# Turning the merged halves in 32 wide blocks: SyncE moves them, VectorE turns them, TensorE no longer does

## What is computed

```python
for l in range(2):
    h = rms_norm(x, mix_norm_g[l])
    z = h @ w_in[l]
    y_a = gmlp_branch(...) @ gm_w_proj[l]
    y_b = mla_branch(...) @ mla_w_proj[l]
    gates = sigmoid(z[..., OFF_GATE:].reshape(B, S, 2, D))
    merged = gates[..., 0, :] * y_a + gates[..., 1, :] * y_b     # (256, 1024)
    x = x + merged @ w_out[l]
    h2 = rms_norm(x, ffn_norm_g[l])
    x = x + (swiglu(h2, ...) if l % 2 == 0 else moe_swiglu(h2, ...))
```

## Time and profile before

| | us |
|---|---|
| median of 3 runs | 1414.58 |
| lowest, highest | 1413.52, 1414.61 |
| profiled execution | 1415.23 |
| its span, first to last instruction | 1413.5 |
| TensorE busy | 1404.5 (99%) |
| VectorE busy | 1167.7 (83%) |
| ScalarE busy | 950.0 (67%) |
| GpSimd busy | 172.1 (12%) |
| granted TensorE clock, mean | 0.999 |

### The profile page before, as it was taken

The page is one execution under the profiler, slowest core; times in us unless marked ns, Lnnn a source line. Parts: engine busy times, 40 slices in busy tenths (PEclk is TensorE's granted clock), DMA queues, the critical chain, the costliest instruction groups (busy, mean ns, idle before and its releaser), DMA issues.

```text
span 1413.5 us, 19089 instructions
## 1 busy us (share of the span) xinstructions
PE 1404.5 (99%) x6567; PEld 1159.6 (82%) x6567; DVE 1167.7 (83%) x1197; ACT 950.0 (67%) x966; POOL 172.1 (12%) x305
## 2 busy tenths in 40 slices
PE   9999999999999999999999999999999999999998
PEld 7888778888888888788888888888888888888886
DVE  6998766676557899667989898898988988999986
ACT  6678645445435677644777777777777777778774
POOL 2032003476600050000300000000000000000010
PEclk9999999999999999999999999999999999999999
DMA  9476549976666484558999999999999999999995
GB/s 338 163 217 207 179 150 332 300 228 201 200 222 206 155 245 128 194 179 314 330 355 410 365 396 408 373 390 405 351 410 372 385 405 365 393 371 393 409 374 188
DMA packets 171636, 424.32 MB, mean 300 GB/s; under 512 B 19436, under 2 KB 50792, under 8 KB 171544
## 3 DMA queue, kind: packets, MB, share of 16 engines
q1 hardware_dynamic: 157128, 393.42, 76.7%
q0 software_dynamic: 13376, 26.16, 6.1%
q10 hardware_dynamic: 1040, 3.68, 0.6%
HBM read 398.20 MB, written 15.81 MB: 293 GB/s over the span
## 4 chain that ended last, share of the span: by engine, by line
PE 96%; DMA 2%; DVE 1%; ACT 0%; SPq 0%; issue 0%; DVEq 0%; ACTq 0%
PE ps L619 89%; DMA raw_more<-in_moe_w_down 1%; PE ps L1194 1%; PE ps L1053 1%; PE ps L1062 1%; PE ps L932 1%; PE ps L1051 1%; PE ps L1037 1%; PE ps L1010 0%; PE ps L976 0%; DMA raw<-in_w_in 0%; DVE w_lo L554 0%; ACT w_hi L549 0%; PE ps L1035 0%; PE ps L1186 0%; SPq L537 0%
## 5 line engine op out<-in xcount | busy, mean ns | idle before, releaser
L554 DVE TENSOR_TENSOR w_lo<-raw,w_hi 128x2048 fp32r<-128x2048 f32 (+3 forms) x184 | 383.7, 2092 | 78.0 <-ACT w_hi L549 76.9
L549 ACT ACTIVATE w_hi<-raw 128x2048 fp32r<-128x2048 f32 (+3 forms) x184 | 322.2, 1758 | 123.7 <-PE ps L619 97.5
L619 PE MATMUL ps<-w_hi,act_hi 128*128 128x512 f32 (+1 forms) x1264 | 332.4, 391 | 0.6 <-DVE w_hi L1803 0.5
L619 PE MATMUL ps<-w_hi,act_lo 128*128 128x512 f32 (+1 forms) x1264 | 328.5, 387 | 0.0
L619 PE MATMUL ps<-w_lo,act_hi 128*128 128x512 f32 (+1 forms) x1264 | 326.8, 387 | 0.0
L619 PEld LDWEIGHTS ps<-w_lo,act_hi 128*128 128x128 f32 x1264 | 235.8, 188 | 48.2
L619 PEld LDWEIGHTS ps<-w_hi,act_lo 128*128 128x128 f32 x1264 | 235.6, 188 | 48.0
L619 PEld LDWEIGHTS ps<-w_hi,act_hi 128*128 128x128 f32 x1264 | 233.1, 188 | 46.9 <-ACT act_hi L1337 1.2
L554 DVE TENSOR_TENSOR w_lo<-raw_more,w_hi 128x2048 fp32r<-128x2048 f32 (+1 forms) x96 | 201.8, 2110 | 30.4 <-ACT w_hi L549 30.4
L549 ACT ACTIVATE w_hi<-raw_more 128x2048 fp32r<-128x2048 f32 (+1 forms) x96 | 170.0, 1775 | 56.1 <-PE ps L619 46.8
L554 DVE TENSOR_TENSOR w_lo<-raw_low,w_hi 128x2048 fp32r<-128x2048 f32 (+1 forms) x64 | 137.6, 2156 | 13.4 <-ACT w_hi L549 12.7
(11 more groups left out here) (296 smaller groups left out, 1353.3 us busy)
## 6 DMA issues: line engine op xcount, KB each, us to landing
raw<-in_moe_w_gu SPq DMA_DIRECT2D x96, 512.0 KB, 11.7
raw_more<-in_moe_w_down SPq DMA_DIRECT2D x80, 512.0 KB, 10.9
raw<-in_w_in SPq DMA_DIRECT2D x66, 512.0 KB, 5.4
raw_low<-in_moe_w_gu SPq DMA_DIRECT2D x64, 512.0 KB, 12.1
raw_more<-in_moe_w_gu SPq DMA_DIRECT2D x64, 512.0 KB, 12.3
raw<-in_moe_w_gu SPq DMA_DIRECT2D x48, 384.0 KB, 8.4
raw<-in_dense_w_gu SPq DMA_DIRECT2D x34, 512.0 KB, 5.3
raw_lent<-in_moe_w_gu SPq DMA_DIRECT2D x32, 512.0 KB, 11.3
```

What stands on the lines that cost most here:

```text
L549: nc.scalar.activation(w_hi[:, self.split_slot(j), 0:n], self.raw(j)[:, 0:n], ACT.Copy).then_inc(self.hi, 1)
L554: nc.vector.tensor_tensor(w_lo[:, c, 0:n], self.raw(j)[:, 0:n], w_hi[:, c, 0:n].bitcast(F32), ALU.subtract).then_inc(self.lo, 1)
L619: return nc.tensor.matmul(dst, a, b, start=start and n == 0, stop=stop and n == 2)
```

## The change

- The sum that makes the merged half (L2013) is written by two instructions, one for each 128 positions, into the space of `u_buf` instead of `vbuf`, its columns in an order in which 32 neighbouring channels, which belong to one block of partitions after the turn, lie together.
- SyncE moves a half into the space of `qb` with 16 DMAs, one for each pair of 32-partition blocks, 32 KB each in pieces of 1 KB. The moves stand in SyncE's queue ahead of the load of the chunk two (half 0) and four (half 1) behind `w_out`'s third. The second also waits until the first half is turned.
- VectorE turns the moved half in blocks of 32x32 with one instruction of 128x1024 (`merged_blocks`), ScalarE copies it to `act_hi` and VectorE makes `act_lo` in two instructions each (`merged_split`). In the plan `merged_blocks` 0 takes the place of `merged_turns` 0; its split stands behind the second chunk of `pb` 1, ahead of that strip's evacuation. Both steps of half 1 stand behind the first chunk of `w_out`'s strip 1.
- TensorE's 16 transposes a layer go. Before `w_out` strip 0 it waits for `m_hi`, before the second pass for `m_lo`.
- The factor 0.5 goes from the copies to the addition to x.
- GpSimd's zeros wait for the second turn, and the loads into the lower slots of the experts' ring for the last low part.

```diff
@@ -130,6 +130,7 @@
     strip_no = 0
     strip_at, chunk_end = {}, {}
     keys_in = {}
+    moves_at = {}
 
     def mul(l, what, j, k0=0, then=(), split=True, inside=()):
 
@@ -153,6 +154,8 @@
             n = min(4, kt - k0)
             h = n // 2
             chunks.append(([(0, h, v[:, k0:k0 + h, :]), (h * width, n - h, v[:, k0 + h:k0 + n, :])], n, width))
+        if (what, k0) == ("wo", 4):
+            moves_at[l, j] = len(chunks) - 1
         if what == "u" or (what, j) in (("gb", 1), ("pa", 0), ("ga", 1)):
             keys_in.setdefault(l, []).append(len(chunks) - 1)
         chunk_end[l, what, j] = len(chunks)
@@ -230,10 +233,10 @@
         mul(l, "pa", 1, 4, [evac("pa", 1)], inside=[(4, ("values", l, PAIRS - 1))])
         mul(l, "pb", 0)
         mul(l, "pb", 0, 4, [evac("pb", 0)])
-        mul(l, "pb", 1, 0, [("merged_turns", l, 0)])
-        mul(l, "pb", 1, 4, [evac("pb", 1)])
-        mul(l, "wo", 0, 0, [("merged_turns", l, 1)] + [("router", l)] * (l % 2))
-        mul(l, "wo", 1)
+        mul(l, "pb", 1, 0, [("merged_blocks", l, 0)])
+        mul(l, "pb", 1, 4, [("merged_split", l, 0), evac("pb", 1)])
+        mul(l, "wo", 0, 0, [("router", l)] * (l % 2))
+        mul(l, "wo", 1, 0, [("merged_blocks", l, 1), ("merged_split", l, 1)])
         mul(l, "wo", 0, 4, [evac("wo", 0), ("split", l, len(chunks)), ("squares", l, 0, 0), ("squares", l, 0, 1)],
             split=False)
 
@@ -380,6 +383,9 @@
         qb = sb("qb", [P, TT, DG, H, 32], F32, mixer)
         kb = sb("kb", [P, TT, DG, H, 32], F32, mixer)
         vv = sb("vv", [P, TT, H, DV], F32, mixer)
+        merged_by_block = u_buf[:].rearrange("p j t n -> p j (t n)").rearrange("p j (c t k i) -> p j c t k i", c=4, t=TT, k=4)
+        merged_moved = qb[:].rearrange("p t g h d -> p (t g h d)")[:, 0:4 * STRIP].rearrange("p (j n) -> p j n", j=2)
+        merged_turned = merged_moved.rearrange("p j (b t k i) -> p j b t k i", b=4, t=TT, k=4)
         ws_t = sb("ws_t", [P, NG, P], F32, mixer)
         prob = sb("prob", [P, 768], F32, mixer)
         prob_t = sb("prob_t", [P, 768], F32, mixer)
@@ -474,6 +480,7 @@
         q_turned, k_turned, q_scaled = sem("q_turned"), sem("k_turned"), sem("q_scaled")
         scores_done, max_ready, exp_done, prob_ready = (
             sem("scores_done"), sem("max_ready"), sem("exp_done"), sem("prob_ready"))
+        m_moved, m_turned, m_hi, m_lo = sem("m_moved"), sem("m_turned"), sem("m_hi"), sem("m_lo")
         merged_b, sig_done = sem("merged_b"), sem("sig_done")
         router_ready, routed_by_pe, routed_by_act = sem("router_ready"), sem("routed_by_pe"), sem("routed_by_act")
         LOGITS_DONE, LOGITS_TURNED, PLACES_DONE = 1, 2, 3
@@ -528,8 +535,7 @@
                     sp.wait_ge(self.lo, last_users[j][0] + 1)
                 elif self.n0:
 
-                    wait_turn_read(sp, last_turn["merged_turns", L - 1, 1])
-                    wait_turn_read(sp, last_turn["merged_turns", L - 1, 1] - 1)
+                    sp.wait_ge(m_lo, 2 * L)
 
             def load(self, sp, e, j, pieces):
                 self.wait_slot(sp, e, j)
@@ -626,7 +632,7 @@
 
 
         def turns_in(step):
-            return {"norm_turns": 2, "latent_turns": 2 - step[2] if step[0] == "latent_turns" else 0, "spatial_weights": 2, "mix_tokens": 2, "merged_turns": 2,
+            return {"norm_turns": 2, "latent_turns": 2 - step[2] if step[0] == "latent_turns" else 0, "spatial_weights": 2, "mix_tokens": 2,
                     "a_turns": 2, "values": 1, "prob_turns": 2}.get(step[0], 0)
 
         def routed(step):
@@ -672,7 +678,7 @@
                     "ukv": lambda: last_turn["latent_turns", l, 1],
                     "pa": lambda: last_turn["a_turns", l, half],
                     "pb": lambda: last_turn["values", l, 4 * half + 3],
-                    "wo": lambda: last_turn["merged_turns", l, half]}.get(what, lambda: None)()
+                    }.get(what, lambda: None)()
 
         def turned_q(head):
 
@@ -743,6 +749,15 @@
                     ring.load(sp, 0, n, [(to[:, 0:half], pieces[1]), (to[:, half:2 * half], pieces[2])])
                 else:
                     ring.load(sp, 0, n, [(v[:, c // w:c // w + kk, :], src) for c, kk, src in pieces])
+
+            def move_merged(l, j):
+                sp.wait_ge(merged_b, 2 * l + j + 1)
+                if j:
+                    sp.wait_ge(m_turned, 2 * l + 1)
+                for b in range(4):
+                    for c in range(4):
+                        sp.dma_start(merged_turned[32 * c:32 * c + 32, j, b, :, :, :],
+                                     merged_by_block[32 * b:32 * b + 32, j, c, :, :, :]).then_inc(m_moved, 16)
 
             for n in range(2):
                 load_x(n)
@@ -757,7 +772,10 @@
                 sp.dma_start(rows[row_at[i]:row_at[i] + row_sizes[i], :], src).then_inc(rows_landed, 16)
             sp.dma_start(consts[:, P:CW], shape_consts[:, P:CW]).then_inc(consts_landed, 16)
             sp.dma_start(causal[:], shape_consts[:, CW:CW + 2 * P]).then_inc(mask_landed, 16)
+            moves = {at + 2 + j: (l, j) for (l, j), at in moves_at.items() if l < L - 1}
             for n in range(RAW, N0):
+                if n in moves:
+                    move_merged(*moves[n])
                 static_load(n)
 
             def rows_load(q, e):
@@ -774,6 +792,8 @@
                 for c in range(GU_CHUNKS):
                     w, to = EG_CHUNKS[c][2], r.raw(c)
                     g, u = expert_gu_pieces(moe_w_gu[0, e], c)
+                    if not q and is_first(e) and c in (0, 2):
+                        move_merged(L - 1, c // 2)
                     r.load(sp, e, c, [(to[:, 0:w], g), (to[:, w:2 * w], u)])
                 for d in range(len(EDOWN_K)):
                     if not last and d == (ROWS_AT if q or not is_first(e) else FIRST_ROWS_AT):
@@ -867,7 +887,7 @@
                 move_heads(k_blocks[1], kb, slice(8, H), k_moved[1])
                 if not l:
 
-                    pool.wait_ge(merged_b, 2)
+                    pool.wait_ge(m_turned, 2)
                     zeros = ws_raw[:].rearrange("p g t -> p (g t)")
                     nc.gpsimd.memset(zeros, 0.0).then_inc(ident_ready, 1)
                     pool.wait_ge(ident_ready, 4)
@@ -1015,12 +1035,6 @@
                     pe.wait_ge(branch_a, 2 * l + j + 1)
                     for b in range(2):
                         turn4(b0 + b, lambda k, t: vbuf[:, t, (4 * j + 2 * b + k) * P:(4 * j + 2 * b + k + 1) * P])
-                elif kind == "merged_turns":
-                    half = step[2]
-                    pe.wait_ge(merged_b, 2 * l + half + 1)
-                    for b in range(2):
-                        c = 4 * half + 2 * b
-                        turn4(b0 + b, lambda k, t: vbuf[:, t, (c + k) * P:(c + k + 1) * P])
                 elif kind == "values":
                     n = step[2]
                     wait_turn_read(pe, prob_turn[l, n])
@@ -1068,7 +1082,10 @@
                     n = strip_at[l, what, j]
                     operand = operand_turns(l, what, k0) if j == 0 else None
                     tiles_first = (what, j, k0) == ("wo", 1, 4)
+                    merged = what == "wo" and not j
                     if not first:
+                        if merged:
+                            pe.wait_ge(m_hi, 2 * l + k0 // 4 + 1)
                         if operand is not None:
                             pe.wait_ge(turn_hi, hi_no[operand] + (c >= 2))
                         if n >= 2 and k0 == 0:
@@ -1096,6 +1113,8 @@
                                 pe.wait_ge(first_lo, c + 1)
                             elif at == 20:
                                 ring.take_lo(pe, 0, c)
+                        elif p == 1 and not cell and merged:
+                            pe.wait_ge(m_lo, 2 * l + k0 // 4 + 1)
                         elif p == 1 and not cell and operand is not None:
                             wait_turns_split(operand + 1)
                         elif p == 2 and not cell:
@@ -1416,10 +1435,13 @@
                 elif kind == "a_turns":
                     for b in range(2):
                         turn_hi_parts(b0 + b, t1_hi, 4 * step[2] + 2 * b, 1.0)
-                elif kind == "merged_turns":
-
-                    for b in range(2):
-                        turn_hi_parts(b0 + b, act_hi, 4 * step[2] + 2 * b, 0.5)
+                elif kind == "merged_split":
+                    j = step[2]
+                    act.wait_ge(m_turned, 2 * l + j + 1)
+                    for t in range(TT):
+                        op = copy(act_hi[:, 4 * j:4 * j + 4, t * P:(t + 1) * P].rearrange("p k (b i) -> p k b i", b=4),
+                                  merged_turned[:, j, :, t].rearrange("p b k i -> p k b i"))
+                    op.then_inc(m_hi, 1)
                 elif kind == "hidden_turn":
                     j = step[2]
                     act.wait_ge(hid_turned, inner_strips(l, j))
@@ -1863,9 +1885,19 @@
                     for b in range(2):
```

(25 more changed lines are left out.)

## The result

The changed kernel takes 1442.41 us, the kernel before 1414.59 us: the ratio is 1.0195, with a 95% interval of 1.0182 to 1.0208. Forecast were 1424.0 us and a range up to 1432. The direction was right, the size was a third of what came. The profiled execution of after took 1442.18 us, its span is 1440.4, 26.9 us longer than that of before.

The account below looks back on a forecast made before the run. TensorE was taken to bound the kernel; waits for the moved halves, less the removed transposes, cost 4.7 us a layer, +9.4 us in all: 1424.6 us profiled, 1424.0 us median. The 8-in-10 range was 1417.5 to 1432 us.

Parts of the forecast that it names:

- What bounds the kernel: Around the merge in both layers: TensorE alone, busy 1404.5 of 1413.5 us, so waits there are paid in full.
- what is removed: Two groups of 8 TensorE transposes a layer, 0.87 us each: 1.74 us a layer, 3.5 us in the kernel.
- The issue of a move: SyncE issuing each of a half's 16 DMAs: 0.37 us with the gap between issues, ends 0.29 and 0.49.
- The landing: Time for a half's last move to land: 2.0 us, between 1.6 and 3.1 us of GpSimd's moves.
- M: Time to move one half by SyncE's 16 DMAs, issue plus landing: 7.65 us, with ends 6.0 and 10.4 us.
- The formula 2M - 10.6: Microseconds a layer ends later, transposes already taken off; M is one half's move time: 4.7 us a layer.
- 0.65 us before wo00's second pass: TensorE's further wait in w_out's first chunk, until VectorE has half 0's low parts ready at 221.2.
- Rival 2: TensorE's clock falls to half in the waits; about 2 us in each layer makes 1428 us; chance 0.17.
- Rival 3: The move crawls, sharing SyncE's queue with weights in flight: 10.4 us a move, 1435 us; chance 0.12.
- Rival 1: The cover holds: TensorE never waits if a move takes at most about 4.4 us; 1411.1 us; chance 0.06.
- What I cost at nothing: SyncE's later loads, VectorE's waits, zero fill, raw_low loads and factor 0.5: no cost, covers such as 8 us.

Follow-up runs that it names:

- the best variant: Against the kernel before, only half 0 uses the 16 moves, issued by SyncE, GpSimd and ScalarE; half 1 still turned by TensorE: 1413.39 us, ratio 0.9990.

## Why the prediction was wrong, point by point

- **What bounds the kernel** and what is removed: right. The transposes' 0.87 us of half 0 was there in full at wo00's start as soon as no wait took its place (half 0 on three engines); wo00's second pass then gave half of it back.
- **The issue of a move, the term that failed.** I took 0.33 + 0.04 us from the nearest row by shape, SyncE's 32-partition copy out of DRAM, with GpSimd's 0.49 for the same kind of move as the upper end. Measured is 0.59 in the median, a pitch of 0.63. The better neighbour was the row of the same kind (SBUF to SBUF), not the row of the same engine, and even that was no upper end. Nothing supported the belief that SyncE can't be dearer than GpSimd for the same move.
- **The landing** of 2.0 us was right (the last issue starts at 217.9 and lands at 219.77, 1.8 us). So M was 11.4 us instead of 7.65, 15 x 0.26 us more of issue (half 1's in layer 0 was 12.0). Four such moves on the path are 15 us of the 18.4 us by which the forecast was short; the clock's 4.4 us, which the sum held at nothing, more than cover the rest.
- **The formula 2M - 10.6 held to less than a microsecond.** With M = 11.4 it gives 12.2 us a layer; measured were 12.2 and 11.4. With the moves as they were it gives 12.8 and 12.0. With the true M and no clock term the forecast would have been 1439.
- **0.65 us before wo00's second pass** did not come, because the first pass ran at the lower clock and the low parts were there. At the full clock a wait of this kind does come: 0.4 us with the moves on two engines, 0.3 us in the best variant.
- **Rival 2, the clock,** was given 0.17 because the wait was reckoned at 3.6 us. Behind all four waits of 5.5 us it came. Its price was 1.5 and 2.8 us; I had written about 2 a layer. The length of the wait alone doesn't say whether it comes: with three engines wo00 fell to 0.50 in layer 0 behind a wait of 2.1 us; with two engines and the router's steps later wo04 kept 1.00 in layer 0 behind one of 2.6. The Trainium skill (TensorE: Matmul & The Clock Gate, Part 1) has the rule behind it, that idleness throttles and sustained work releases, and here the trace agrees: 0.50 granted behind each of the four waits, 1.00 again 3 to 6 us into the work.
- **Rival 3** named the right symptom, a pitch over 0.45 us, and the wrong cause. It laid the crawl to weights in flight. SyncE's issues were at 0.59 us with the DMA engines idle for most of the time (their share is 0.13 to 0.25 in each microsecond from 209 to 219), and M went beyond the 10.4 us at which I had closed the range.
- **Rival 1** was too kind. The cover of half 1 does not hold at an M near 4.4: with four moves (4.1 us for half 0) VectorE's split of wo14's weights and the router's step stand ahead of the turn. My sum had followed VectorE's row for half 0 and not for half 1.
- **What I cost at nothing** stayed at nothing: SyncE's later loads, the zero fill, raw_low's loads, the factor 0.5. GpSimd once waited 23.8 us for the zero fill ahead of the hidden blocks' moves, and nobody waited for GpSimd.

## What to carry to other kernels

Price a DMA that is issued many times by its issue, taken from a row with the same source and destination kind and the same engine, and where there is none take the range well past the dearest neighbour; from 16 to 128 KB neither bytes nor shape moved the price here. Splitting the issues over engines helps as far as those engines have nothing queued behind them that the critical path wants: read each lent queue for the wait that comes with it and for the loads that it was carrying. Where TensorE is made to wait as long as here, 5.5 us, price the matmuls behind the wait at half the clock, but only where no other path is later.

## What the runs showed that was not expected

- SyncE takes 0.59 us to issue an SBUF to SBUF move, against 0.33 us for a copy out of DRAM with 32 partitions, and ScalarE about the same (0.62 us). It is 0.59 for 16 KB and for 32 KB, 0.60 for 128 KB on 128 partitions. GpSimd takes 0.50 us for the same move and is the cheapest of the three.
- 60 transposes of 128x128 in TensorE's row are 6.71 us, 0.11 us each, as the earlier trace rows had it for 8.
- The landing of an SBUF to SBUF move spreads: 1.8 us in the median for 32 KB, up to 3.8; 2.4 us for 128 KB, up to 6.1 in layer 1, where router and weight loads were issued beside it.
